# Tile 1 merged and routed alone, tiles 2 to 4 as one group, and the slots' sums on two PSUM banks

## What is computed

```python
# end of sub-layer 1
merged = (gates[0] * (oa @ w_o_a) + gates[1] * (ob @ w_o_b) + gates[2] * (oc @ w_o_c))
x = x + g1 * (merged @ w_out)
# sub-layer 2, a block of 128 tokens
h = rmsnorm(x, g_ffn_norm) * (1 + sc2) + sh2
q = (h @ w_pq).reshape(t, 8, 2, 128)
sc = einsum('thpd,hpkd->thpk', q, keys)              # 8 heads x 2 halves x 128 keys
sv, si = top_k(sc, 16)                               # 16 first choices per head and half
cv, ci = top_k(sv[:, :, 0, :, None] + sv[:, :, 1, None, :], 16)   # 16 of 256 pairs per head
gate = softmax(cv)
act = gelu(einsum('thkd,td->thk', u_tab[eidx], h))   # 128 rows of 4 KB per token
x = x + g2 * einsum('thk,thkd->td', gate * act, v_tab[eidx])
```

## Time and profile before

| | us |
|---|---|
| median of three runs | 5154.03 |
| lowest and highest | 5147.48, 5154.66 |
| span of the profiled execution | 5145.4 |
| TensorE busy in it | 3978.3 (77%) |
| VectorE busy | 2905.9 (56%) |
| ScalarE busy | 1635.7 (32%) |
| GpSimd busy | 1556.1 (30%) |

### The profile page before, as it was taken

How to read it: one execution, slowest core, us unless ns; L and a number is a source line. 1 busy time by engine, 2 the same in 40 slices (tenths; PEclk the granted TensorE clock), 3 DMA queues, 4 the chain that set the end, 5 groups by cost and what they waited for, 6 DMA issues and landing times.

```text
span 5145.4 us, 62465 instructions
## 1 busy us (share of the span) xinstructions
PE 3978.3 (77%) x20366; PEld 1626.3 (32%) x20366; DVE 2905.9 (56%) x6315; ACT 1635.7 (32%) x4867; POOL 1556.1 (30%) x1453
## 2 busy tenths in 40 slices
PE   5988899778887666666679889997788887666666
PEld 3555653332223211111134556533322232111111
DVE  3543544675666676654445434446756667766544
ACT  0211542223333333333322115422233333333333
POOL 0210012233334444343312100132333344444432
PEclk8989999988999977666779899998889998677666
DMA  7126049899999999999941260498899999999998
GB/s 281 48 78 236 7 167 399 344 339 372 421 406 409 420 421 421 421 421 421 421 183 48 99 221 1 179 398 340 341 373 421 411 409 413 421 421 421 421 421 357
DMA packets 232449, 1640.19 MB, mean 319 GB/s; under 512 B 26688, under 2 KB 28864, under 8 KB 36800
## 3 DMA queue, kind: packets, MB, share of 16 engines
q0 software_dynamic: 184320, 1342.26, 63.8%
q1 hardware_dynamic: 47808, 293.94, 15.0%
HBM read 1632.82 MB, written 3.28 MB: 318 GB/s over the span
## 4 chain that ended last, share of the span: by engine, by line
PE 37%; DMA 35%; DVE 17%; issue 5%; ACT 4%; DVEq 2%; POOL 1%; SPq 0%; ACTq 0%; POOLq 0%
DMA arena<-in_experts,arena 30%; PE ps L751 12%; PE ps L985 8%; DVE sq L1455 6%; DMA front<-in_experts,arena 3%; PE ps L936 3%; PE ps L961 3%; DMA arena<-in_weights 2%; PE ps L888 2%; PE ps L949 2%; PE ps L913 2%; PE ps L900 1%; ACT arena L1122 1%; DVE arena L1185 1%; DVE negm L1346 1%
## 5 line engine op out<-in xcount | busy, mean ns | idle before, releaser
L985 PE MATMUL ps<-arena 64*64 64x512 f32 x9040 | 1569.3, 777 | 828.2 <-ACT arena L1122 813.5
L724 POOL DMA_INDIRECT arena<-in_experts,arena x1130 | 1261.1, 1116 | 2774.9 <-PE ps L985 1891.6
L1455 DVE CUSTOM_DVE_ANT_0 sq<-arena 128x1024 f32<-128x1024 f32 x1130 | 1386.1, 1227 | 909.4 <-DMA arena<-in_experts,arena 831.3
L985 PEld LDWEIGHTS ps<-arena 64*64 64x64 f32 x9040 | 312.8, 156 | 1923.1 <-issue 1900.5
L1116 ACT ACTIVATE arena<-arena 128x1 f32<-128x1 f32 x1280 | 258.4, 202 | 2073.9 <-DVE arena L1455 2058.2
L751 PE MATMUL ps<-arena 128*128 128x512 f32 (+3 forms) x1920 | 819.3, 574 | 21.9 <-DMA arena<-in_weights 20.0
L1122 ACT ACTIVATE arena<-ident,arena 128x128 f32<-128x128 f32 x1280 | 513.9, 402 | 91.8 <-issue 3.4
L751 PEld LDWEIGHTS ps<-arena 128*128 128x128 f32 x1920 | 360.3, 195 | 467.5 <-issue 427.0
L1118 ACT ACTIVATE arena<-arena 128x1 f32<-128x1 f32 x1280 | 376.7, 294 | 92.1 <-issue 5.2
L961 PE MATMUL ps<-arena 128*128 128x256 f32 (+1 forms) x1536 | 349.3, 372 | 6.3 <-issue 2.3
L961 PEld LDWEIGHTS ps<-arena 128*128 128x128 f32 x1536 | 251.7, 199 | 183.4 <-issue 150.5
(11 more groups left out here) (159 smaller groups left out, 3039.4 us busy)
## 6 DMA issues: line engine op xcount, KB each, us to landing
arena<-in_weights SPq DMA_DIRECT2D x242, 1024.0 KB
arena<-in_experts,arena POOLq DMA_INDIRECT x1130
arena<-mod_rows SPq DMA_DIRECT2D x24, 512.0 KB, 7.1
arena<-in_weights SPq DMA_DIRECT2D x8, 576.0 KB
arena<-in_keysT SPq DMA_DIRECT2D x4, 1024.0 KB, 12.9
arena<-in_g_norm SPq DMA_DIRECT2D x6, 512.0 KB, 9.4
arena<-in_weights SPq DMA_DIRECT2D x4, 768.0 KB
arena<-in_weights SPq DMA_DIRECT2D x6, 512.0 KB
```

The source lines that it names most:

```text
L724: pool.indirect_dma_start(out=ring[BUF[n]], out_offset=None, in_=ins["experts"], in_offset=bass.IndirectOffsetOnAxis(ap=index(t)[:, slot:s ...
L985: last = MM(acc[h][to:to + 64, c * 512:(c + 1) * 512], diag[n % 4][lo:lo + 64, lo:lo + 64], ring[BUF[n]][lo:lo + 64, D + c * 512:D + (c + ...
L1455: V.tensor_tensor_reduce(out=sq[:], in0=ring[BUF[n]][:, 0:D], in1=h2_of_slot(n), scale=1.0, scalar=0.0, op0=ALU.mult, op1=ALU.add, accum_o ...
```

## The change

Three things are changed. The groups become tile 1 alone and tiles 2, 3 and 4 together, and the line places tile 1's merge and route on slots -3 to 70 and those of tiles 2 to 4, with the choice for tile 2 inside the route, on slots 70 to 248; tile 3's choice goes to 262 to 340. The sum of a slot holds one bank for each row half, in which the two column halves lie on different partitions, so that banks 2 to 7 are free for other products. And the places in SBUF follow: `hT` of tile 1 moves behind that of tile 4, so that tiles 2 to 4 are adjacent, the merged rows of tile 4 lie where `hT` of tile 1 was, query and score buffers are 384 wide for the group of three, and row buffer 6 is released by the last query product of group 2.

```diff
-GROUPS = {0: (0,), 1: (1, 2), 2: (3, 4)}
+GROUPS = {0: (0,), 1: (1,), 2: (2, 3, 4)}
...
-        line.spread(-3, 118, pieces(merge(l, 1) + route(l, 1, 1)))
-        line.spread(140, 236, choose(l, 2))
-        line.spread(118, 320, pieces(merge(l, 2) + route(l, 2)))
-        line.spread(322, 372, choose(l, 3))
+        line.spread(-3, 70, pieces(merge(l, 1) + route(l, 1, 1)))
+        line.spread(70, 248, pieces(merge(l, 2) + route(l, 2, 2)))
+        line.spread(262, 340, choose(l, 3))
...
-        ACC_BEFORE[_it[1]] = sorted({h for b in range(4) for h in _held[b]})
+        ACC_BEFORE[_it[1]] = sorted({h for b in range(2) for h in _held[b]})
...
-        _take(_it, min((4, 6) if _open else (2, 4, 6), key=lambda b: max(_used[b:b + 2])), 2)
+        _take(_it, min((2, 4, 6), key=lambda b: max(_used[b:b + 2])), 2)
...
-        _take(_it, min(range(4, 8) if _open else range(2), key=lambda b: _used[b]), 1)
+        _take(_it, min(range(2, 8) if _open else range(2), key=lambda b: _used[b]), 1)
...
-RELEASE = {6: lambda l: ("pq", l, 1, 15), 7: lambda l: ("pq", l, 2, 15), 8: lambda l: ("o", l, NT - 1, 1),
+RELEASE = {6: lambda l: ("pq", l, 2, 15), 7: lambda l: ("pq", l, 2, 15), 8: lambda l: ("o", l, NT - 1, 1),
...
+        hT_at = lambda t: HT0 + D * (0, 4, 1, 2, 3)[t]
...
-        merged = lambda t: scr(0, D) if t == 0 else at(8192 + D * GROUPS[GROUP_OF[t]].index(t), D)
+        merged = lambda t: scr(0, D) if t == 0 else ar(hT_at(1), D) if t == 4 else at(8192 + D * (t == 3), D)
...
-        acc = [ps[:, 2 * h:2 * h + 2, :].rearrange("p a n -> p (a n)") for h in range(2)]
+        acc = [ps[:, h, :] for h in range(2)]
...
-                            last = MM(acc[h][to:to + 64, c * 512:(c + 1) * 512], diag[n % 4][lo:lo + 64, lo:lo + 64],
+                            last = MM(acc[h][to:to + 64, :], diag[n % 4][lo:lo + 64, lo:lo + 64],
...
-                    if kind == "hT1" and l and t in (1, 3):
-
-                        act.wait_ge(slot_used, FINAL_IN[l - 1, 6 + t // 2] + 1)
+                    if kind == "hT1" and l and t in (1, 2):
+
+                        act.wait_ge(slot_used, FINAL_IN[l - 1, 8 - t] + 1)
...
-                    A(cross[0:64, 0:512], acc[1][0:64, 512:D], ACT.Copy)
-                    out(A(cross[64:128, 0:512], acc[0][64:128, 512:D], ACT.Copy))
+                    A(cross[0:64, 0:512], acc[1][0:64, :], ACT.Copy)
+                    out(A(cross[64:128, 0:512], acc[0][64:128, :], ACT.Copy))
...
-                    TT(sq[0:64, 0:512], acc[0][0:64, 0:512], g2[0:64, 0:512], ALU.mult)
-                    TT(sq[64:128, 0:512], acc[1][64:128, 0:512], g2[64:128, 0:512], ALU.mult)
+                    TT(sq[0:64, 0:512], acc[0][0:64, :], g2[0:64, 0:512], ALU.mult)
+                    TT(sq[64:128, 0:512], acc[1][64:128, :], g2[64:128, 0:512], ALU.mult)
```

More of the change, by code:

```diff
@@ L319 @@
         _open = True
-        ACC_BEFORE[_it[1]] = sorted({h for b in range(4) for h in _held[b]})
+        ACC_BEFORE[_it[1]] = sorted({h for b in range(2) for h in _held[b]})
     elif _k == "ew" and _it[2] == NT - 1:
         _open = False
-        for _b in range(4):
+        for _b in range(2):
             _held[_b] = (("ea",) + _it[1:], ("ex",) + _it[1:])
@@ L482, in build @@
         wring = [ar(W0 + r * UNIT, UNIT) for r in range(NU)]
-        hT = lambda t: ar(HT0 + D * t, D).rearrange("p (k n) -> p k n", k=DK)
-        hT_of = lambda ts: ar(HT0 + D * ts[0], D * len(ts)).rearrange("p (t k n) -> p t k n", t=len(ts), k=DK)
+        hT_at = lambda t: HT0 + D * (0, 4, 1, 2, 3)[t]
+        hT = lambda t: ar(hT_at(t), D).rearrange("p (k n) -> p k n", k=DK)
+        hT_of = lambda ts: ar(hT_at(ts[0]), D * len(ts)).rearrange("p (t k n) -> p t k n", t=len(ts), k=DK)
         kaT = arena[0:AQK, R0:R0 + 7168].rearrange("p (h t) -> p h t", h=H)
@@ L517, in build @@
         oT = lambda t: zt(t)[:, 0:1536].rearrange("p (k n) -> p k n", k=12)
-        merged = lambda t: scr(0, D) if t == 0 else at(8192 + D * GROUPS[GROUP_OF[t]].index(t), D)
+        merged = lambda t: scr(0, D) if t == 0 else ar(hT_at(1), D) if t == 4 else at(8192 + D * (t == 3), D)
         sg = lambda j, t: scr(1024 + 512 * (j % 2), 512) if t == 0 else at(18432 + 512 * (j % 2), 512)
-        pqb = lambda gid, q: scr(2048 + P * (q % 2), P) if gid == 0 else at(17408 + 256 * (q % 2), 256)
-        scb = lambda gid, q: scr(2304 + P * (q % 2), P) if gid == 0 else at(17920 + 256 * (q % 2), 256)
+        pqb = lambda gid, q: scr(2048 + P * (q % 2), P) if gid == 0 else at(17408 + 128 * (q % 2), 128) if gid == 1 else at(17408 + 384 * (q % 2), 384)
+        scb = lambda gid, q: scr(2304 + P * (q % 2), P) if gid == 0 else at(17664 + 128 * (q % 2), 128) if gid == 1 else at(18176 + 384 * (q % 2), 384)
         rows2 = [[at((13442, 12288)[c] + D * j, D) for j in range(3)] for c in range(2)]
```

## The result

The changed kernel takes 5357.7 us (median of four runs, 5355.0 to 5362.6) where the kernel before takes 5153.0 beside it: a ratio of 1.0401, 95% interval 1.0386 to 1.0416. That is 205 us slower; 82 were forecast. The profiled span grew from 5145.4 to 5357.4.

The account below looks back on a forecast made before the run. The prediction took DMA's fixed bytes plus its idle time in slots 0 to 320 as the bound. Five stages, 138 + 143 + 367 + 265 + 163 = 1076 us against 1036 and 1034, gave 5154 + 82 = 5236 us, range 5180 to 5300.

Parts of the forecast that it names:

- The bound: Whole layer: DMA's bytes are fixed; only its idle time in slots 0 to 320, some 87 us, can change.
- the prices: Engine costs: on TensorE a part 1.72 us, a slot 1.21; on VectorE a dot product 1.36, a first top-16 1.93.
- What costs nothing: Two-bank sums, shared bank reads, later row buffers and earlier weight units: no cost expected beyond what the stages count.
- A: Slot products on TensorE: column halves in one bank run one after the other, +125 us a layer, about 5486; chance 0.05.
- C: Routes and new merge: free banks remove all waits between engines, -11 us a layer, 5132 in all; chance 0.07.
- B: Slots 0 to 320: stalls shrink, VectorE keeps its bare sum in half the stages; no change, 5154 us; chance 0.08.
- Step (1): Merge of tile 1, slots 0 to 32: set by DMA, 138 us (134 to 147).
- Step (2): Route of tile 1, slots 32 to 70: VectorE's sum of 132 us, 143 with waits (132 to 148).
- Step (3): Merge of tiles 2 to 4, slots 70 to 170: set by TensorE, 367 us (350 to 378), DMA partly idle.
- Step (4): Route of tiles 2 to 4 with tile 2's choice, slots 170 to 248: VectorE, 265 us with waits (248 to 285).
- The sign given for this stage: Slots 170 to 248 should take some 265 us with VectorE busy near 80%.
- Step (5): Slots 248 to 320, no weights left: DMA's 181 us less rows lying ready, 163 us (156 to 181).

Follow-up runs that it names:

- e1: Kernel before, old grouping and line, with only a slot's sums moved to two PSUM banks, six left for other products: 5149.5 us, ratio 0.9997.
- e2: Changed kernel, new grouping and line, but sums on four banks and four for the rest as before: 5363.2 us, ratio 1.0416 to the kernel before.
- e4: Changed kernel with half of the products of the gates of tiles 2 to 4 left out: 5302.5 us, ratio 1.0295 to the kernel before.
- e5: Changed kernel with each first top-16 placed one query later, same work: 5260.7 us, ratio 1.0212 to the kernel before.
- e7: Changed kernel with tile 1's choice moved out of its route, beside the merge of tiles 2 to 4: 5265.3 us, ratio 1.0222 to the kernel before.
- e8: Changed kernel with first top-16 one query later and tile 1's choice beside the merge of tiles 2 to 4: 5173.9 us, ratio 1.0049.

## Why the prediction was right in kind and wrong in size

**The bound and the prices held.** DMA's bytes are fixed, the loss is its idle time in slots 0 to 320, and after slot 320 the two kernels keep nearly the same pace: slots 320 to 639 took 5 us longer in layer 0 and 4 in layer 1. A slot and a part on TensorE cost what they did, to the hundredth in e1, and a slot with one part took 1107.57 - 1104.63 = 2.94 us in the changed kernel's merge. "What costs nothing" held as far as it was run: the banks (e1, e2). The later release of row buffer 6 was not run by itself, but VectorE waited only 13.0 us for rows in the merge of tiles 2 to 4 and 3.5 us in their route. Rivals A and C are refuted. B is refuted by the result itself. One sum is off without weight: the high ends add up to 1139, not 1141.

**Step (1)** was 6 and 4 us short. The stage is DMA's, as said: 1.01 share at 420 GB/s. But 145 us at 420 GB/s are 58 transfers of 1.05 MB, not 53. By the trace's bytes 34.6 gathers and 22.6 units came in (32.4 and 21 in the sum): at the stage's end TensorE stands 8.1 us for the norm while the DMA engines go on at 421 GB/s and fill row buffers and weight ring. That fill was left out of the sum.

**Step (2)** held: 144 and 143 against 143. VectorE's bare sum of 132 and 13.2 us of waits for scores make 145.

**Step (3)** held nearly: 375 and 378 against 367; the plain sum, 378, without the ratio of 0.972 from the old merge, would have been better. That TensorE set the gates' and projections' part is shown by e4.

**Step (4) failed**, and carries two thirds of the miss: 304 and 308 against 265. The bare sum of VectorE, 248, was right: 248 and the 52.9 us of waits are 301. What was wrong is the term for waits, and with it the premise that a stage is about as long as its slowest engine. I put 17 us on the bare sum, 7% where the old route had 8%, or a little over 1 us for each score; measured were (52.9 - 10.4)/14 = 3.0 us each, without the first. In the old route the same pair also made 15 waits, (22.1 - 8.9)/14 = 0.9 us each; that price did not carry over to three tiles. Two numbers of the prediction together might have warned: it puts VectorE's bare sum at 248 and TensorE's at 220 for the same stage. Both are near the whole, and each engine's order makes it wait for the other's last step. Why a wait is three times as long with three tiles as with two, no run separates. The upper end, 285, came from that same route's pace and was too low for the same reason. The sign given for this stage also failed: VectorE was busy 70% of it, not 80%. That the waits were the missing term is shown, not argued: e5 changes only the order, takes 50 us of waits away, and the stage falls to 260, near the 265 of the forecast. In all, e5 lands at 5261, inside the range that the prediction gave.

**Step (5)** held: 166 and 167 against 163; the rows that lay ready were there.

Summed over both layers the steps miss by 57 + 62 = 119 us, step (4) alone by 39 + 43 = 82. With the 82 that were forecast, 119 make 201 of the 205 measured; the rest is below the spread of the runs.

**Why the change costs time at all** is argued from the stages; e2 shows only that the grouping and its line carry the loss. Before, tiles 3 and 4 had until slot 384 for their choices and lay thinly under the transfers. In the new grouping their queries share products with tile 2's, so everything up to the last score must be done by slot 248. The work that was hidden is now denser than the transfers beside it. e7 and e8 show that part of it can be hidden by pairing a TensorE stage with VectorE's steps; not all.

Not tried: a longer distance between a dot product and its slot's product, which might loosen the stop at each second norm.

## What to carry to other kernels

Where two engines feed each other within a stage, the stage can be longer than the slower one's sum. If the two sums are close, as 248 and 220 were here, look at how far apart the list places a result and its use, and price one wait per round, not a share of an old one. Moving a consumer one round later cost a few lines and was worth 97 us in one grouping and 22 in the other. And before work is grouped, ask which deadline the group inherits: the earliest member's.

## What the runs showed of the hardware

That 64 x 64 products whose column halves share a PSUM bank, on different partitions, keep the pace of separate banks (2.93 us for a slot and a part in both, ratio 0.9997, e1) was priced as likely and is now measured; the prediction had no row for it. The two extra free banks did nothing even in the densest merge, as was priced: with four banks in place of six (e2) the ratio to the kernel before is 1.0416 against 1.0401, and the intervals overlap.
